# First x tile of a boundary from prescaled parts, its h made later

## The reference

```python
for i in range(DEPTH):
    f = swiglu(rmsnorm(h, P['g_f1_pre'][i]), P['w_f1_gate'][i], P['w_f1_up'][i], P['w_f1_down'][i])
    h = h + 0.5 * rmsnorm(f, P['g_f1_post'][i])
    mo, a1, a2, a3 = mixer(rmsnorm(h, P['g_mix_pre'][i]), bpool[i], bsc[i], bcf[i], pos0, P, i)
    h = h + rmsnorm(mo, P['g_mix_post'][i])
    f = swiglu(rmsnorm(h, P['g_f2_pre'][i]), P['w_f2_gate'][i], P['w_f2_up'][i], P['w_f2_down'][i])
    h = h + 0.5 * rmsnorm(f, P['g_f2_post'][i])
    gate = jax.nn.sigmoid(rmsnorm(h, P['g_ple_pre'][i]) @ P['w_ple_gate'][i])
    h = h + rmsnorm((p[i] @ P['w_ple_proj'][i]) * gate, P['g_ple_post'][i])
```

## Time and profile before

| what | value |
|---|---|
| median of 3 runs | 1541.18 us (1539.96 to 1541.54) |
| the profiled execution's own time | 1541.55 us |
| its span, first to last instruction | 1539.9 us |
| mean granted TensorE clock | 0.995 |
| TensorE busy | 1525.8 us (99%) |
| VectorE busy | 1034.3 us (67%) |
| ScalarE busy | 720.5 us (47%) |
| GpSimd busy | 654.0 us (42%) |
| chain that ended last | 96% TensorE |

### The profile page before, as it was taken

How to read it: one execution, slowest core, us unless ns; L and a number is a source line. 1 busy time by engine, 2 the same in 40 slices (tenths; PEclk the granted TensorE clock), 3 DMA queues, 4 the chain that set the end, 5 groups by cost and what they waited for, 6 DMA issues and landing times.

```text
span 1539.9 us, 27992 instructions
## 1 busy us (share of the span) xinstructions
PE 1525.8 (99%) x10361; PEld 1518.3 (99%) x10361; DVE 1034.3 (67%) x1589; ACT 720.5 (47%) x1086; POOL 654.0 (42%) x695
## 2 busy tenths in 40 slices
PE   9999999999999999999999999999999999999997
PEld 9999999999999999999999999999999999999997
DVE  7655437999886755533885554389998866555347
ACT  6333336445466433433753334354554664334356
POOL 2855203499331565500147551045973307554012
PEclk9999999999999999999999999999999999999998
DMA  6545432444443544533334454334444335445422
GB/s 220 169 158 181 180 129 83 164 139 163 151 161 110 187 149 151 186 144 117 125 123 166 148 194 177 119 110 138 152 151 163 121 137 187 156 143 188 150 82 82
DMA packets 54281, 229.30 MB, mean 149 GB/s; under 512 B 3776, under 2 KB 6208, under 8 KB 49856
## 3 DMA queue, kind: packets, MB, share of 16 engines
q1 hardware_dynamic: 53632, 226.07, 42.9%
q10 hardware_dynamic: 576, 2.26, 0.4%
HBM read 225.27 MB, written 3.04 MB: 148 GB/s over the span
## 4 chain that ended last, share of the span: by engine, by line
PE 96%; issue 2%; DVE 1%; POOL 1%; ACT 0%; DVEq 0%; POOLq 0%; ACTq 0%
PE ps L504 29%; PE ps L506 29%; PE ps L505 29%; PE ps L546 2%; PE ps L542 2%; PE ps L543 2%; PE ps L668 1%; PE ps L580 1%; PE ps L572 1%; PE ps L571 1%; PE ps L617 0%; PE ps L609 0%; PE ps L636 0%; POOL x_lo L1765 0%; ACT win L1249 0%
## 5 line engine op out<-in xcount | busy, mean ns | idle before, releaser
L1271 DVE TENSOR_TENSOR w_lo_sb<-raw,w_hi_sb 128x1024 fp32r<-128x1024 f32 (+1 forms) x384 | 546.2, 1424 | 219.8 <-ACT w_hi_sb L903 218.9
L903 ACT ACTIVATE w_hi_sb<-raw 128x1024 fp32r<-128x1024 f32 (+1 forms) x384 | 424.7, 1112 | 546.6 <-PE ps L506 445.7
L504 PE MATMUL ps<-x_hi,w_hi_sb 128*128 128x320 f32 x2176 | 674.2, 310 | 0.8 <-DVE w_lo_sb L1271 0.8
L505 PE MATMUL ps<-x_lo,w_hi_sb 128*128 128x320 f32 x2176 | 671.9, 309 | 0.0
L506 PE MATMUL ps<-x_hi,w_lo_sb 128*128 128x320 f32 x2176 | 671.9, 309 | 0.0
L504 PEld LDWEIGHTS ps<-x_hi,w_hi_sb 128*128 128x128 f32 x2176 | 408.5, 188 | 2.7 <-issue 1.3
L505 PEld LDWEIGHTS ps<-x_lo,w_hi_sb 128*128 128x128 f32 x2176 | 408.6, 188 | 0.3
L506 PEld LDWEIGHTS ps<-x_hi,w_lo_sb 128*128 128x128 f32 x2176 | 408.5, 188 | 0.0
L506 PE MATMUL ps<-mid_hi,w_lo_sb 128*128 128x320 f32 x704 | 217.4, 309 | 0.0
L504 PE MATMUL ps<-mid_hi,w_hi_sb 128*128 128x320 f32 x704 | 217.4, 309 | 0.0
L505 PE MATMUL ps<-mid_lo,w_hi_sb 128*128 128x320 f32 x704 | 217.4, 309 | 0.0
(11 more groups left out here) (244 smaller groups left out, 1720.8 us busy)
## 6 DMA issues: line engine op xcount, KB each, us to landing
raw<-in_w_f_up SPq DMA_DIRECT2D x84, 1024.0 KB, 5.3
raw<-in_w_f_dn SPq DMA_DIRECT2D x32, 1408.0 KB, 5.9
raw<-in_w_gate SPq DMA_DIRECT2D x24, 1024.0 KB, 5.3
raw<-in_w_out SPq DMA_DIRECT2D x12, 1024.0 KB, 5.3
raw<-in_w_glu SPq DMA_DIRECT2D x8, 1024.0 KB, 5.3
raw<-in_w_short SPq DMA_DIRECT2D x8, 1024.0 KB, 5.2
raw<-in_w_wo SPq DMA_DIRECT2D x8, 1024.0 KB, 5.3
raw<-in_w_pg SPq DMA_DIRECT2D x8, 1024.0 KB, 5.2
```

The costliest lines, as they stand in the source:

```text
L504: pe.matmul(out, whi, rhs_hi, start=start, stop=False, skip_group_check=True)
L505: pe.matmul(out, whi, rhs_lo, start=False, stop=False, skip_group_check=True)
L903: act.activation(w_hi_sb[:, j, 0:n], src[:, 0:n], ACT.Copy).then_inc(w_hi, 1)
L1271: dve.tensor_tensor(w_lo_sb[:, j, 0:n], src[:, 0:n], w_hi_sb[:, j, 0:n].bitcast(F32), ALU.subtract).then_inc(w_lo, 1)
```

## The change

At the boundaries n = 0, 1 and 2 the first x tile is no longer made from the new h. Ahead of the last output of the sublayer, ScalarE (`first_ahead`) multiplies `f` of tile 0 and the old h of tile 0 by the pre gain, into the two halves of `gb`, here called `AHEAD_F` and `AHEAD_H`. When `bc` is there, VectorE (`first_x`) makes `AHEAD_F * bc` in PSUM and adds `AHEAD_H` twice: once into `x_hi` of tile 0, once into `pmf`, from which GpSimd makes `x_lo`. ScalarE's `scaled` for tile 0 goes. The new h of tile 0 is still needed: its step and its addition now stand behind h of tile 4, and ScalarE's square of it behind the square of tile 4. Boundary 3 stays as it was.

```diff
--- before.py
+++ after.py
@@ -213,6 +213,8 @@
         halves_done = sem("halves_done")
         moved = sem("moved")
         squared = sem("squared")
+        ahead = sem("ahead")
+        x0_step = sem("x0_step")
         last_sq_head = sem("last_sq_head")
         f_out = sem("f_out")
         summed = sem("summed")
@@ -407,6 +409,14 @@
 
         POST4_ALONE = (5, 6)
 
+        CHASE = (1, 2, 3, 4, 0, 5, 6, 7)
+
+        def h_at(n, m):
+
+            return (CHASE.index(m) if n < 3 else m) + 1
+
+        AHEAD_F, AHEAD_H = gb[:, 0, :], gb[:, 1, :]
+
         TAILED = ("post1", "post2", "post3", "post4")
 
 
@@ -945,6 +955,15 @@
                 act.wait_ge(proj_done, L * DT + q + 1)
                 act.activation(gate[:, q, :], ps[:, PROJ_BANKS[q], 0:T], ACT.Copy).then_inc(early_act if q < EARLY else proj_act, 1)
 
+            def first_ahead(L, n, gain):
+
+                c = cur[:, COL[gain]:COL[gain] + 1]
+                if n != 1:
+                    act.wait_ge(mid_ready, (L * 2 + (1 if n == 0 else 2)) * FT + 2)
+                act.wait_ge(f_out, v_f(L, n, 0))
+                act.activation(AHEAD_F, f[:, 0, :], ACT.Copy, scale=c).then_inc(ahead, 1)
+                act.activation(AHEAD_H, h[:, 0, :], ACT.Copy, scale=c).then_inc(ahead, 1)
+
             def scaled(L, n, m, gain):
 
                 if m == 2:
@@ -956,13 +975,16 @@
 
                 if n == 2:
                     keep_product(L, EARLY)
-                act.wait_ge(h_ready, L * 4 * DT + n * DT + 1)
-                scaled(L, n, 0, gain)
+                if n == 3:
+                    act.wait_ge(h_ready, L * 4 * DT + n * DT + 1)
+                    scaled(L, n, 0, gain)
                 if n == 1:
                     keep_product(L, MIXER + 1)
+                done = 0
+                order = CHASE if n < 3 else range(DT)
                 for m in range(1, DT + 1):
                     if m < DT:
-                        act.wait_ge(h_ready, L * 4 * DT + n * DT + m + 1)
+                        act.wait_ge(h_ready, L * 4 * DT + n * DT + h_at(n, m))
                         if n == 0 and over_weights(m, MIXER_W):
                             act.wait_ge(proj_done, L * DT + MIXER)
                         if n == 2 and over_weights(m, PROJ):
@@ -974,8 +996,10 @@
                         if m == 1 and n == 1:
                             keep_product(L, MIXER + 2)
                     else:
-                        act.wait_ge(h_ready, L * 4 * DT + n * DT + m)
-                    act.activation(CHASE_SQ[m - 1], h[:, m - 1, :], ACT.Square).then_inc(squared, 1)
+                        act.wait_ge(h_ready, L * 4 * DT + n * DT + DT)
+                    while done < DT and (order[done] < m and (n == 3 or order[done] or m > 4)):
+                        act.activation(CHASE_SQ[done], h[:, order[done], :], ACT.Square).then_inc(squared, 1)
+                        done += 1
                 if n == 0:
                     act.wait_ge(proj_done, L * DT + MIXER)
                     for q in (1, 0):
@@ -1025,6 +1049,8 @@
             def down_step(L, ph, nxt, pair, prev_pair, name, gain, last=False):
                 for j in range(4):
                     if j >= 2:
+                        if j == 3 and last:
+                            first_ahead(L, 0 if name == "post1" else 2, "g_mix_pre" if name == "post1" else "g_ple_pre")
                         act.wait_ge(halves_done, v_half(L, ph, prev_pair, j) + 4)
                         if j == 3 and last:
                             last_output(ps[:, 1, 0:T], L, name, DT - 1, 1, gain, (L, nxt, pair))
@@ -1199,6 +1225,8 @@
                         if (pair, j) == (0, 1):
                             act.wait_ge(early_proj_in, L * 16 + 16)
                             act.activation(early_hi, early_raw, ACT.Copy).then_inc(early_proj_hi, 1)
+                        if pair == 1 and j == 3:
+                            first_ahead(L, 1, "g_f2_pre")
                         act.wait_ge(halves_done, v_half(L, "wo", pair, j) + 4)
                         if pair == 1 and j == 3:
                             last_output(ps[:, 3, 0:T], L, "post2", DT - 1, 1, "g_mix_post", (L, "f2_up", 0))
@@ -1318,16 +1346,27 @@
                 steps = [ps[:, b, 0:T] for b in STEP_BANKS[n]]
 
                 def step(i):
-                    if i >= len(steps):
-                        dve.wait_ge(h_ready, before + i - len(steps) + 1)
-                    dve.tensor_tensor(steps[i % len(steps)], (f if n < 3 else gate)[:, i, :], bc, ALU.mult).then_inc(step_t, 1)
+                    k = h_at(n, i) - 1
+                    if k >= len(steps):
+                        dve.wait_ge(h_ready, before + k - len(steps) + 1)
+                    if n < 3 and k == 1:
+                        dve.wait_ge(gh_ready, v_pool_x(L, n, 0))
+                    dve.tensor_tensor(steps[k % len(steps)], (f if n < 3 else gate)[:, i, :], bc, ALU.mult).then_inc(step_t, 1)
 
                 def new_h(i):
-                    dve.wait_ge(step_t, before + i + 1)
+                    k = h_at(n, i) - 1
+                    dve.wait_ge(step_t, before + k + 1)
                     if n < 3:
-                        dve.tensor_tensor(h[:, i, :], h[:, i, :], steps[i % len(steps)], ALU.add).then_inc(h_ready, 1)
+                        dve.tensor_tensor(h[:, i, :], h[:, i, :], steps[k % len(steps)], ALU.add).then_inc(h_ready, 1)
                     else:
-                        ple_h(i, steps[i % len(steps)])
+                        ple_h(i, steps[k % len(steps)])
+
+                def first_x():
+                    dve.wait_ge(ahead, (L * 3 + n) * 2 + 2)
+                    dve.tensor_tensor(steps[1], AHEAD_F, bc, ALU.mult).then_inc(x0_step, 1)
+                    dve.wait_ge(x0_step, L * 3 + n + 1)
+                    dve.tensor_tensor(x_hi[:, 0, :], steps[1], AHEAD_H, ALU.add).then_inc(x0_hi, 1)
+                    dve.tensor_tensor(SCALED_H[0], steps[1], AHEAD_H, ALU.add).then_inc(gh_ready, 1)
 
                 def x_low(m):
                     if m == 0:
@@ -1350,10 +1389,13 @@
                 if n == 1:
                     dve.wait_ge(early_dve, L + 1)
 
-                step(0)
-                new_h(0)
-                dve.wait_ge(h_ready, before + 1)
-                dve.tensor_scalar(x_hi[:, 0, :], h[:, 0, :], cur[:, g:g + 1], None, ALU.mult).then_inc(x0_hi, 1)
+                if n < 3:
+                    first_x()
+                else:
+                    step(0)
+                    new_h(0)
+                    dve.wait_ge(h_ready, before + 1)
+                    dve.tensor_scalar(x_hi[:, 0, :], h[:, 0, :], cur[:, g:g + 1], None, ALU.mult).then_inc(x0_hi, 1)
                 step(1)
                 new_h(1)
                 for i in range(2, DT):
@@ -1361,6 +1403,9 @@
                     new_h(i)
                     if i - 1 not in POOL_X:
                         x_low(i - 1)
+                    if n < 3 and i == 4:
+                        step(0)
+                        new_h(0)
                 x_low(DT - 1)
                 split(*nxt, 3)
                 if n == 2:
```

## The result

| | before | changed |
|---|---|---|
| median, us | 1541.12 (1539.76 to 1541.54, 16 runs) | 1543.60 (1542.65 to 1546.33, 16 runs) |
| ratio | | 1.0021, 95% interval 1.0015 to 1.0027 |
| the profiled execution's own time | 1541.55 | 1542.77 |
| its mean granted clock | 0.995 | 0.997 |

What follows compares the result with a forecast made beforehand. TensorE, busy nearly all of the span, was taken as the bound. Losses of 2.31 us in layer 0 and 2.04 in layer 1, rounded 4.4 together, on a median of 1541.18 gave 1545.6 us, range 1542.6 to 1548.0.

Steps and rivals of the forecast that it cites:

- Early scalings, x_hi 0: Ahead of the sublayer's last output, two ScalarE scalings cost nothing; at the boundary's start x_hi 0 is done 0.42 us earlier.
- The `step_t` wait: GpSimd at boundary 0 waits for step 1, so TensorE gets x_lo 0 0.3 us late instead of 0.2 early.
- The pair: VectorE's step 0 and h 0 between h 4 and step 5 take 0.93 us; h 5, 6, 7 come 0.91 late.
- ScalarE's square: Tile 0's square behind tile 4's adds 0.36 us on ScalarE, making x_hi 6 and x_lo 6 1.27 late.
- no hole to put the square in: ScalarE's pieces stand back to back, so none of the square is taken up and the upper delay, 1.27 us, holds.
- the same formula: TensorE's loss at x_lo 6: delay less slack plus 0.10; 0.63, 0.41 and 0.61 us at boundaries 0, 1 and 2.
- The sums of boundary 2: TensorE's sums of squares follow x_hi 7's delay: 1.27 us late in layer 0, 1.0 in layer 1.
- The sum: Losses on TensorE's path over six boundaries: 2.31 us in layer 0 and 2.04 in layer 1, together 4.35.
- the square is taken up: Rival: ScalarE absorbs the square, x_hi 6 is late only by VectorE's 0.91; 1.8 us slower, 1543.0 us; chance 0.09.
- Later tiles stay covered: Rival: x_lo 6's delay stays under 0.74 us, kernel not slower; 1540.0 to 1541.2 us; chance 0.04.
- The clock rival: New TensorE waits at the boundaries lower its granted clock, six times 1.2 us; 1553 us; chance 0.07.

Runs made afterwards that it cites:

- e1: The changed kernel, but GpSimd at boundary 0 waits for the multiply of tile 0, not for step 1; ratio to before 1.0016.
- e3: The changed kernel, but step and h of tile 0 stand behind h of tile 7 on VectorE, their square last on ScalarE; ratio to before 1.0000.
- e4: The changed kernel with the edits of e1 and e3 together; ratio to before 0.9998.
- e7: The kernel before, plus two unused VectorE instructions between x_lo 3 and step 5 at boundaries 0, 1 and 2; ratio to before 1.0016.
- e9: The kernel before, plus two unused VectorE instructions behind x_lo of tile 7 at boundary 0 only; ratio to before 1.0004.
- second run: The changed kernel measured again, unedited, beside other kernels; +3.1 us against before at either clock, ratio 1.0020.
- e2: The changed kernel, but ScalarE squares h of tile 0 last, behind the square of tile 7; ratio to before 1.0019.

## Why the prediction was right, and where its sizes were off

**Early scalings, x_hi 0.** Right: the two scalings cost nothing (at boundary 1 ScalarE still waits 0.82 behind them, of 1.72), x_hi 0 is 0.42 earlier, and the waits for it are gone.

**The `step_t` wait.** Right in place and size: 0.37 from release to start, TensorE 0.30 late at x_lo 0 (3.11 behind the first multiply, 2.81 before). As said, it does not show in the end while x_lo 6 is later (e1). It does in e3: 0.29, where e4 removes it. At boundaries 1 and 2 TensorE has x_lo 0 only 0.12 and 0.10 earlier, not 0.19, and this does not show in the end either.

**The pair.** 0.92 for 0.93; x_hi 5 0.91 late, as forecast.

**ScalarE's square.** Mis-sized. x_hi 6 is 1.17 late, not 1.27: behind x_hi 5 the first square starts 0.47 later, the second 0.36 and x_hi 6 again 0.36. Forecast were 0.47, 0.36 and 0.46. The step that was off is "no hole to put the square in": the 0.46 from the square to x_hi 6 in rows 3 held a wait for h 6. VectorE's h 6, before and changed:

```profile
250.50 0.49 DVE L1328 TENSOR_TENSOR h<-h,ps 128x320 f32<-128x320 f32 x1
```

```profile
250.62 0.49 DVE L1360 TENSOR_TENSOR h<-h,ps 128x320 f32<-128x320 f32 x1
```

Before, h 6 ends at 250.99 and x_hi 6 starts 0.03 later. Now h 6 ends at 251.11 and x_hi 6 starts 0.29 later, 0.36 behind the square in front of it: ScalarE had a hole of 0.10 and put as much of the square there. With the 1.16 by which x_lo 6 is late, the same formula gives 1.16 - 0.74 + 0.10 = 0.52 for boundary 0 and 0.50 for boundary 2. At boundary 1, where VectorE's first multiply also comes 0.08 later behind the first sum, x_lo 6 is 1.22 late, which gives 0.36. Measured were 0.51, 0.37 and 0.50 against 0.63, 0.41 and 0.61 forecast.

**The sums of boundary 2.** Mis-sized most: 0.88 for 1.27 in layer 0, 0.49 for 1.0 in layer 1. VectorE behind the last tile of h, layer 0, in the changed kernel, and TensorE's sums:

```profile
740.33 0.55 DVE L1377 SCALAR_TENSOR_TENSOR x_lo<-h,cur,x_hi 128x320 fp32r<-128x320 f32 x1 [0.82 <-ACT x_hi L992]
740.80 1.91 DVE L1299 TENSOR_TENSOR w_lo_sb<-raw,w_hi_sb 128x1024 fp32r<-128x1024 f32 x1
...
743.90 1.58 DVE L1417 TENSOR_TENSOR ssq<-ssq,cc 128x320 f32<-128x320 f32 x2
745.52 0.49 DVE L1421 TENSOR_TENSOR ssq<-ssq,bg 128x320 f32<-128x320 f32 x1
```

```profile
746.06 0.83 PE L627 MATMUL ps<-ones_r,ssq 128*128 128x1 f32 x6 [0.30 <-DVE ssq L1421]
```

Counted from the first sum (726.22 before, 726.75 now), x_lo 7 starts 1.04 late (ahead of x_hi 7 ScalarE takes up a second 0.1 of the square), but takes 0.55 where it took 1.21. Before, GpSimd's first square had started 0.02 ahead of it (738.74); now it starts 0.09 behind it:

```profile
740.42 1.20 POOL L1816 TENSOR_TENSOR bg<-bg 128x320 f32<-128x320 f32 x1
```

So the split starts only 0.38 late. GpSimd's third square (743.62) then lies beside VectorE's two sums, which take 1.58 instead of 1.09, and the last add is 0.88 late. I had passed the 1.27 through unchanged and not looked at what runs beside each piece. In layer 1:

```profile
1508.14 0.49 DVE L1421 TENSOR_TENSOR ssq<-ssq,bg 128x320 f32<-128x320 f32 x1
```

```profile
1508.88 0.73 PE L627 MATMUL ps<-ones_r,ssq 128*128 128x1 f32 x6
```

There the add is 0.88 late too, but with 0.64 of slack before and TensorE 0.51 late by x_lo 6, 0.25 are left: the chain does not count at all, and the 0.49 is x_lo 6's.

**A term that was missing.** VectorE's debt in layer 0's mixer, 0.24 to 0.33 (e7, e9). I had followed the pair to the end of the boundary and no further.

**The sum.** Measured (second run), with boundary 1 of layer 1 taken as in layer 0: 0.50 + 0.37 + 0.88 + 0.52 + 0.37 + 0.49 = 3.13, and 0.33 in the mixer: 3.5, against 4.35 forecast and 3.1 to 3.2 in the runs. The forecast is 1.2 too high at the six boundaries, 0.9 of it in the sums, and 0.33 too low in the mixer, so the errors offset each other in part, which is luck. The remaining 0.3 can't be placed: start-up and single holes differ by as much between executions (before's boundary 1 in layer 1 had one of 0.35, which the changed kernel's execution has not).

**The rivals.** The median of 1543.60 lies nearer to the 1543.0 of "the square is taken up" than to 1545.6, and the range holds both: the time alone does not choose. The traces do: x_hi 6 is 1.17 late, where that rival needs 0.91, and by e2 0.26 of the square's 0.36 is felt there. "Later tiles stay covered" falls with the four waits for x_lo 6 and with e1, where x_lo 0 comes 0.49 earlier and boundary 0 ends where it did. That TensorE would wait for x_lo 6 at all six boundaries came true at four; at boundary 0 the listed wait is that for x_lo 0. The clock rival falls for the boundaries: TensorE waited there up to 0.82 and kept a granted clock of 1.00, and where the clock was lowered, it was at the boundary between the layers and at the end, in before as well. Ahead of that fall TensorE had run short products, as I wrote, but before's trace shows no wait there: it was busy for 4.00 of the 4.00 us from 764.

## What to carry to other kernels

Taking work off the head of a chain is worth only what the next link allows, here x_lo 2. Work that is put off must go where its engine is idle: behind tile 7 the same pair costs nothing that these runs can tell (e3: 0.9991 to 1.0009), behind tile 4 it costs some 3 us, since everything behind it on a busy engine is late. Pieces that stand close on an engine can still hide a wait: ScalarE's x_hi 6 looked back to back with the square in front and had waited 0.10 for its h. And a debt on a busy engine does not end with its stage: look for the next place where another engine asks for its output, even 100 us on.

## What the runs showed of the hardware

VectorE's pieces with two SBUF operands can take longer while GpSimd works. In the kernel before, x_lo 7 at boundary 2 took 1.21, where GpSimd's square had started 0.02 ahead of it and took 0.88:

```profile
738.74 0.88 POOL L1771 TENSOR_TENSOR bg<-bg 128x320 f32<-128x320 f32 x1
```

In the changed kernel x_lo 7 started 0.09 ahead of the square; then x_lo 7 took 0.55 and the square 1.20. In these two cases the piece that started first kept its time. The Trainium skill, "SBUF — State Buffer", section "Who interferes with whom", has a Vector instruction with two SBUF inputs contend with a GpSimd instruction that reads SBUF, and calls the port pair that they share "an exclusive lock". The trace agrees in kind; the 0.66 added to x_lo 7 is less than the square's 0.88.

ScalarE's pieces start 0.09 to 0.10 before the end of the piece in front, where they wait for nothing: in the changed kernel 0.46 to 0.47 behind an x_hi (0.55 to 0.56 long), 0.36 behind a square (0.45 to 0.46).

The granted clock in the stretch ahead of the second layer is kept in some executions and lowered in others of the same kernel; a lowered one costs 1.1 to 1.5 us (before, its runs beside the experiments). What decides it stays open.
